# One-hots of the expert selection: every third block of four tokens on GpSimd instead of VectorE and ScalarE

## What is computed

```python
def peer_ffn(h, w_q, sub_keys, u_tab, v_tab):
    q = (ht @ w_q).astype(jnp.float32).reshape(T, PEER_HEADS, 2, PEER_DKEY // 2)
    s = jnp.einsum('thpd,hpkd->thpk', q, sub_keys.astype(jnp.float32))
    s_top, i_top = lax.top_k(s, PEER_TOPK)
    cand_s = s_top[:, :, 0, :, None] + s_top[:, :, 1, None, :]
    cand_i = i_top[:, :, 0, :, None] * PEER_NKEYS + i_top[:, :, 1, None, :]
    best_s, best_j = lax.top_k(cand_s.reshape(T, PEER_HEADS, -1), PEER_TOPK)
    experts = jnp.take_along_axis(cand_i.reshape(T, PEER_HEADS, -1), best_j, axis=-1)
    gates = jax.nn.softmax(best_s, axis=-1)
    ...
        a = jnp.einsum('tkd,td->tk', u_tab[eb], hb)
        w = (jax.nn.gelu(a.astype(jnp.float32)) * gb).astype(hb.dtype)
        return jnp.einsum('tk,tkd->td', w, v_tab[eb])
```

## Time and profile before

| | us |
|---|---|
| runs | 5753.6, 5748.69, 5750.75 |
| median | 5750.75 |
| span of the profiled execution | 5748.8 |

### The profile page before, as it was taken

One profiled execution on the slowest core, in us unless ns is written; L12 is line 12 of the kernel. 1 busy time (PEld: TensorE's weight loads), 2 busy tenths in 40 slices (PEclk: granted clock), 3 DMA queues, 4 the chain that ended last, 5 costly groups with the idle time before them and its releaser, 6 DMA issues. The chain is left out here.

```text
span 5748.8 us, 69904 instructions
## 1 busy us (share of the span) xinstructions
PE 4806.6 (84%) x23606; PEld 3828.5 (67%) x23606; DVE 4288.4 (75%) x7455; ACT 1811.2 (32%) x3273; POOL 978.5 (17%) x708
## 2 busy tenths in 40 slices
PE   7696737889698778999999867979797559999998
PEld 5395736643576667888888736753576448888886
DVE  1547576867734987999999857757743998999997
ACT  0232311221122563333333320222122464444443
POOL 0000004610000002333333306400000002222221
PEclk9798868989899889999999978989999669999999
DMA  6152316821122468999999918721122149999996
GB/s 230 66 163 83 99 55 232 329 92 55 48 88 94 130 187 330 384 384 385 383 388 384 354 55 321 265 99 40 62 77 77 42 105 344 377 372 377 379 378 254
DMA packets 458724, 1231.49 MB, mean 214 GB/s; under 512 B 210275, under 2 KB 244484, under 8 KB 397382
## 3 DMA queue, kind: packets, MB, share of 16 engines
q1 hardware_dynamic: 357192, 625.56, 31.9%
q0 software_dynamic: 101376, 604.02, 26.7%
HBM read 1169.37 MB, written 60.03 MB: 214 GB/s over the span
## 5 line engine op out<-in xcount | busy, mean ns | idle before, releaser
L2400 POOL DMA_INDIRECT arena<-in_peer_uv,kept x448 | 637.9, 1424 | 3387.4 <-POOLq L2251 1967.0
L233 PE MATMUL psum<-v_ring_hi,w_parts 128*128 128x512 f32 x2560 | 837.7, 392 | 7.6 <-DVE v_lo L2506 7.6
L233 PE MATMUL psum<-h_hi,u_ring_hi 128*128 128x384 f32 (+1 forms) x2048 | 672.5, 328 | 50.4 <-DVE u_lo L2501 50.2
L233 PE MATMUL psum<-h_hi,u_lo 128*128 128x384 f32 (+1 forms) x2048 | 665.4, 325 | 0.0
L233 PE MATMUL psum<-h_lo,u_ring_hi 128*128 128x384 f32 (+1 forms) x2048 | 664.4, 324 | 0.0
L2531 DVE CUSTOM_DVE_ANT_0 arena<-arena 128x1024 f32<-128x1024 f32 x448 | 536.4, 1220 | 51.2 <-DMA arena<-in_peer_uv,kept 50.6
L2541 DVE SCALAR_TENSOR_TENSOR arena<-arena 128x1024 f32<-128x1024 f32 x448 | 558.6, 1282 | 19.2
L233 PEld LDWEIGHTS psum<-v_ring_hi,w_parts 128*128 128x128 f32 x2560 | 482.6, 189 | 104.1 <-DVE v_lo L2506 9.4
L233 PE MATMUL psum<-v_lo,w_parts 128*128 128x512 f32 x1280 | 502.6, 393 | 0.0
L233 PEld LDWEIGHTS psum<-h_hi,u_ring_hi 128*128 128x128 f32 x2048 | 386.5, 189 | 98.3 <-DVE u_lo L2501 48.0
L233 PEld LDWEIGHTS psum<-h_lo,u_ring_hi 128*128 128x128 f32 x2048 | 386.8, 189 | 5.0 <-issue 0.5
(11 more groups left out here) (386 smaller groups left out, 9749.6 us busy)
## 6 DMA issues: line engine op xcount, KB each, us to landing
kept<-in_mix SPq DMA_DIRECT2D x312, 512.0 KB, 3.5
kept<-in_peer_u SPq DMA_DIRECT2D x256, 512.0 KB, 7.0
kept<-in_peer_uv SPq DMA_DIRECT2D x256, 512.0 KB, 5.8
kept<-in_ada SPq DMA_DIRECT2D x96, 512.0 KB, 4.3
gate_scratch<-arena SPq DMA_DIRECT2D x11, 4096.0 KB, 20.8
arena<-gate_scratch SPq DMA_DIRECT2D x64, 384.0 KB, 5.9
arena<-gate_scratch SPq DMA_DIRECT2D x64, 320.0 KB, 8.5
spec_scratch<-arena SPq DMA_DIRECT2D x4, 2048.0 KB, 8.5
```

The source lines that it names most:

```text
L233: done = pe.matmul(out, lhs[x], rhs[y], start=first and j == 0, stop=last and j == 2)
L2400: pool.indirect_dma_start(rows[q % NBUF], None, peer_uv, bass.IndirectOffsetOnAxis(ap=at, axis=0))\
```

## The change

Chunks with n % 3 == 1 (`of_pool`) are made by POOL: 11 of 32, or 5 of 16. DVE and ACT leave them out. For each of the four tokens POOL runs two instructions of 128 elements per partition: one compares `iota` with the row numbers and multiplies by the gate, the other compares it with the column numbers. These chunks always use buffer `hot[1]`, and the others never do. PE waits for a semaphore of POOL's for them, and not for `weigh`. POOL waits for the turned picks of the tile, and for PE to have done chunk n-3. The counts of the other semaphores are taken over the chunks that are left.

```diff
+            def of_pool(n):
+
+                return n % 3 == 1
+
+            def equal_by(t, n):
+
+
+                done = sum(1 for u in range(t) for k in range(chunks_of(u)) if of_pool(k) == of_pool(n))
+                done += sum(1 for k in range(n + 1) if of_pool(k) == of_pool(n))
+                return (pool_equal, done) if of_pool(n) else (equal_ready, done)
...
                     def gates(t, n):
-                        pe.wait_ge(equal_ready.sem, equal_ready.at(CHUNKS * t + n + 1))
-                        pe.wait_ge(weighted.sem, weighted.at(CHUNKS * t + n + 1))
+                        made, count = equal_by(t, n)
+                        pe.wait_ge(made.sem, made.at(count))
+                        if not of_pool(n):
+                            pe.wait_ge(weighted.sem, weighted.at(weighed_before(t, n) + 1))
...
                     def weigh(t, n):
 
-                        act.wait_ge(equal_ready.sem, equal_ready.at(CHUNKS * t + n + 1))
+                        if of_pool(n):
+                            return
+                        made, count = equal_by(t, n)
+                        act.wait_ge(made.sem, made.at(count))
...
+                if dense:
+                    @block.gpsimd
+                    def _(pool):
+                        for t in range(dense):
+                            pool.wait_ge(turned.sem, turned.at(t + 1))
+                            for n in range(chunks_of(t)):
+                                if not of_pool(n):
+                                    continue
+                                pool.wait_ge(pe_b.sem, pe_b.at(max(0, CHUNKS * t + n - 2)))
+                                for q in range(4):
+                                    at = slice(4 * n + q, 4 * n + q + 1)
+                                    pool.tensor_scalar(hot_i[n % 3][:, q, :], iota, picked_t[:, 0, at], weight[:, at], ALU.is_equal, ALU.mult)
+                                    last = pool.tensor_scalar(hot_j[n % 3][:, q, :], iota, picked_t[:, 1, at], None, ALU.is_equal)
+                                last.then_inc(pool_equal.sem, 1)
...
+                            if of_pool(n):
+                                continue
                             dve.wait_ge(pe_b.sem, pe_b.at(max(0, CHUNKS * t + n - 2)))
```

More of the change, by code:

```diff
@@ L105, in build @@
         weighted, equal_ready = new("weighted_hots_ready"), new("equal_hots_ready")
+        pool_equal = new("equal_hots_of_pool_ready")
         pe_c, turned = new("pe_third"), new("picks_turned")
@@ L1865, in chunks_of, with weighed_before @@
                 return CHUNKS // 2 if halved and t == dense - 1 else CHUNKS
+            def of_pool(n):
[4 more added lines that the diff above has]
+                return (pool_equal, done) if of_pool(n) else (equal_ready, done)
+            def weighed_before(t, n):
+                return sum(1 for u in range(t) for k in range(chunks_of(u)) if not of_pool(k))                     + sum(1 for k in range(n) if not of_pool(k))
             def last_exponent(n):
@@ L2180, in stage_select @@
             act_b.add(chunks)
-            weighted.add(chunks)
-            equal_ready.add(chunks)
+            pool_chunks = sum(1 for t in range(dense) for n in range(chunks_of(t)) if of_pool(n))
+            pool_equal.add(pool_chunks)
+            equal_ready.add(chunks - pool_chunks)
+            weighted.add(chunks - pool_chunks)
             turned.add(dense)
```

## The result

| | before | with the change |
|---|---|---|
| median of 4 runs | 5749.72 (5745.23 to 5753.6) | 5872.61 (5861.94 to 5878.96) |
| span of the profiled execution | 5748.8 | 5865.6 |

The ratio is 1.0213, 95% interval [1.0196, 1.023]: 2.1% slower, 123 us. The prediction of 5711 us, faster, was wrong, and so was its range.

The account below looks back on a forecast made before the run. DVE was taken to set layer 1's pace, with layer 0 closer and PE bounding its tile 2. Relief of 57.8 us, less 9 for unevenness and 9.5 for shared reads, gave 39.3 us: 5711 us, range 5690 to 5790.

Parts of the forecast that it names:

- POOL's price: One POOL operation taken as 0.39 us (0.10 to 1.42), eight as 3.1 us a chunk (0.8 to 11.4).
- my own break-even: In layer 1, POOL cancels the gain at 0.71 us an operation; it is hidden up to 0.56.
- the meeting of DVE and POOL: Both engines read the same rows at once: 0.1 us for each of 95 DVE comparisons, 9.5 us deducted.
- Rival 2: DVE's comparisons wait for POOL's eight operations, 0.71 us each, 68 us instead of 9.5: 5770 us; chance 0.18.
- rival 3: POOL waits 2.4 us behind DVE's two comparisons, or operations take 0.65 to 0.85 us: gain lost, 5748; chance 0.14.
- My own rule of the round: On hot[1], three chunks take at least POOL's eight operations plus PE's product (1.13 or 2.05): 4.2 to 5.2 us.
- rival 4: POOL becomes the bound at 1.0 us an operation, three chunks 10.05 us in layer 1: 5850 us; chance 0.12.
- unevenness: Chunks come unevenly, POOL's chunks 1 and 31 at a tile's ends: 1.5 us a tile, 9 us deducted.
- The relief: DVE gives up 1.12 us for each of 60 chunks, 67.2 us; 57.8 us reach the end before deductions.
- the sentence that I would be wrong: The prediction is wrong if POOL's chunk with its waits takes over 5.5 us.
- a sign for layer 0: In the profile after, layer 0's tiles 0 and 1 should take 76 us.

Follow-up runs that it names:

- PSUM input: Changed kernel, but DVE's comparison reads the turned picks from PSUM, so it has one SBUF input: 5769.87 us, ratio 1.0039.
- own copies: Changed kernel, but POOL reads its own copies of iota and the picks elsewhere in SBUF: 5865.55 us, ratio 1.0205.
- every sixth chunk: Changed kernel, POOL making every sixth chunk: 5813.22 us; also with DVE's picks from PSUM: 5748.12; then also chunk 31 left to DVE and ACT: 5727.92.
- nearly free: Changed kernel, but from each tile's second POOL chunk on POOL runs one operation instead of eight: 5702.67 us, ratio 0.9911.
- both cures: Changed kernel, with DVE's comparison reading the picks from PSUM and two buffers for POOL: 5705.82 us, ratio 0.9917.

## Why the prediction was wrong

**The first failed step is POOL's price.** I took 0.39 us an operation from ACT's row and 3.1 us a chunk. Start to start it is 0.78 and 0.59, 5.5 us a chunk, before anything disturbs it. The bounds of 0.10 to 1.42 held the value, but I chose within them by likeness, and both rows that I chose between (0.227 on DVE, 0.386 on ACT) were of engines that aren't POOL. The only rows of POOL's, 0.10 for one element and 1.42 for an indirect DMA, have 0.76 in their middle, and 0.71 was my own break-even. The Trainium skill ("GPSIMD Engine Reference", section "3.1 Elementwise — side-by-side cycle accounting") made it an estimated 0.19 us plus dispatch. For 128 elements the trace has 0.59 at the least, so what comes on top of the 0.19 is some 0.40 us, twice as much.

**The second failed step, the larger one by time, is who waits.** I charged the meeting of DVE and POOL to DVE, 0.1 us for 95 comparisons, 9.5 us. DVE paid almost nothing: its 116 comparisons last 143.5 us, and 140.4 where their input comes from PSUM. POOL paid 1.95 us a chunk (7.45 - 5.5), 1.3 of it to this comparison, and taking that away gave back 103 us. What is left there, 5770 against the forecast 5711, has to be the price, the end of a tile, the stretch by the pick's own instructions and a relief some 8 us smaller; how it divides was not measured. Rival 2 (DVE held up, 5770) thus fell; the mechanism of rival 3 (POOL stands behind DVE's comparisons) was right, nearly in its size of 2.4 us. The Trainium skill ("SBUF — State Buffer", section "Who interferes with whom") says that a DVE instruction with two SBUF inputs contends with a POOL instruction that reads SBUF; the runs agree, PSUM input and own copies included. It also says that who issues first decides; that is not seen here in full: a DVE comparison that started inside a POOL operation (4685.21 against 4684.94 to 4685.74) lasted 1.24 us all the same, and the longest of the 116 lasted 1.41. At what moment of an operation POOL reads, no row shows, so this stays open.

**Rivals aren't exclusive.** Rival 3 asked for 3.1 + 2.4 us or for an operation of 0.65 to 0.85. Its 5748 was worked out from layer 1 alone: by the same rule layer 0 would take 5.5 + 1.13 = 6.6 us and keep its gain, and at 0.85 layer 1 would already lose 27 x 1.15 = 31 us. Both of its conditions came true together: 0.68 an operation on average, 5.5 us a chunk, and 1.95 of stretch. My own rule of the round gives 7.45 + 2.05 = 9.5 us for three chunks in layer 1 (9.13 in the round shown), 1.8 more than before, and 7.45 + 1.13 = 8.6 in layer 0, 0.6 more. That is 27 x 1.8 + 33 x 0.6 = 68 us slower, rival 4's outcome. In layer 0 the rule is too kind: PE didn't keep the high clock there (0.90 became 0.80), and was busy 8.7 and 10.6 us longer a tile. I gave rival 4 0.12, at 1.0 us an operation; with its stretch the operation is 0.93.

**The end of a tile was sized too small.** For unevenness with chunk 31 in it I took 9 us. The waits before the copy rose from 8.7 to 50.8 us, 42. With the 68 that is 110 of the 113 us; it fits in sum, single tiles lie up to 11 us beside it, so the sum is partly luck. That chunk 31 is a cost of its own is shown for every sixth chunk (20 us), not for the change itself.

**What held.** The relief: DVE's tiles of layer 1 fell to 70.2 us where POOL was nearly free, forecast 70.0; there the whole gain was 50 us by the medians of that comparison, forecast 58. The missing part is in layer 0: its two whole tiles gave 5.3 and 7.0 us, not 10.8 each, since PE is busy 66.6 us of the first's 79.9, stood 5.4 for a block's DMA and 7.8 more for POOL, for ACT and without a shown cause; I had let it wait 4.8 in all. The rule of the round held in the two rounds of layer 1 shown above, with the chunk as it was measured (6.9 + 2.05 against 9.13, 5.45 + 2.05 against 7.59), and so did the sentence that I would be wrong if POOL's chunk took over 5.5 us. The 76 us given as a sign for layer 0 didn't follow from my own sum, which makes 74.5 + 1.5 + 2.1 = 78. That the forecast 5711 is nearly the time of both cures (5706) is chance: the terms are others. What is shown is that a gain existed, behind a price that I had guessed.

## What to carry to other kernels

Before work moves to an engine that has done no arithmetic in the trace, its price is the whole question: if the break-even lies inside the bounds, the change is a coin toss, and one small measurement of that operation is worth more than the sum. Look at who shares a buffer and a queue with the slow engine: alone on one buffer it stands in series with its reader, and the last piece of a stage, with the hand-over queued behind it, should stay with the fast one while the slow engine sets the pace (20 us here; nothing once it had a second buffer). And where POOL works beside DVE, give DVE's instructions one input from PSUM where it lies there anyway; here that was worth 103 us and cost nothing.

## What the runs showed of the hardware

- A TENSOR_SCALAR on POOL of 128 partitions x 128 elements with a scalar per partition takes 0.59 us from start to start with one operation and 0.78 with two; the same size takes 0.227 on DVE and 0.386 on ACT. The second operation costs 0.19 us.
- POOL's operations are held up while a DVE instruction with two SBUF inputs runs (0.60 becomes 1.2 to 1.4 under a comparison of 1.2 us; 0.80 becomes 5.0 under one of 4.4). The DVE comparisons are 0.03 us longer on average; 12 of 116 last 1.31 to 1.41 us, where the longest before was 1.23. With one input in PSUM neither is longer: 347 POOL operations beside DVE instructions with at most one SBUF input are longer by 0.14 us at most, and no comparison is over 1.224 us. Separate rows for POOL don't help.
- PE's granted clock fell with its waits: 0.69 in the tiles of layer 1 against 0.75 and 0.77 before, 0.80 in layer 0 against 0.90, and it rose to 0.83 in both tiles of layer 1 with both cures, where PE hardly waited for POOL. A chunk's product is 1.13 us at the high clock (2.4 GHz; the granted clock in that stretch is 1.00) and 2.05 at the low (1.2 GHz; 0.50), so a product that falls into the low clock behind a wait costs 0.9 us more.
